# A decode step with three token mixers on one core: the delta rule's preparation written as one run in the order table

## The chip, the cores and the metric

The kernel runs on one core of a Trainium2 chip. The metric is the device time of one execution in microseconds; lower is better. Times are the median of repeated runs, and one further execution was taken with the hardware profiler. Engines are named as in the profile: PE (TensorE, the matmuls), PEld (its weight loads), DVE (VectorE), ACT (ScalarE), POOL (GpSimd) and SP (SyncE, which here only issues DMAs). TensorE's granted clock has two levels, 1.2 and 2.4 GHz; the profile gives it as a share of full speed, 0.50 or 1.00.

## The reference

One decoder layer is computed for a prompt of 256 tokens and for 8 sampled sequences with one new token each (264 columns in all), D_MODEL 1024. Cut to what matters:

```python
h = rms_norm(x, norm1_w) * (1 + sc1) + sh1            # sc, sh from silu(c) @ ada_w
proj = h @ w_in                                        # 22 chunks of 128 columns, and beta/decay columns
u_pool, q_a, k_a, v_a, q_d, k_d, v_d, z, b_raw, a_raw = split(proj)
y_pool = pool_mixer(u_pool)                            # trailing windows 2/4/8/16
q_a, k_a = rms_norm(q_a, q_norm_w), rms_norm(k_a, k_norm_w)     # per head of 64
y_att = moba_attention(q_a, past_k + k_a, past_v + v_a)         # 8 heads; 1024 cached keys a sample
q, k, v = silu(short_conv(q_d, k_d, v_d)); q, k = l2_norm(q), l2_norm(k)
# gated delta rule, 4 heads: in each chunk, with decay from cumsum(g)
A = I + strict_lower(kbeta @ k.T * decay)              # inverted by the triangular solve
u, kcum = solve(A, v * beta), solve(A, kbeta * exp(gcum))
attn = (q @ k.T) * decay                               # then the state is carried over chunks
x = x + g1 * (concat(y_pool, y_att, y_dn) @ w_out)
x = x + g2 * ((silu(h2 @ w_gate) * (h2 @ w_up)) @ w_down)
```

## The kernel before

Activations stand transposed, 128 features on the partitions and 264 token columns. Large operands pass through a ring of five slots of 1 MB (`ring`): column blocks of the weights, and the cached keys and values in pieces of four pages. SP issues their DMAs in the order in which the items are used, and item number n waits until item n-5 was read.

The middle of the program, between the first modulation and the output projection, is one list of steps, the string `ORDER` (L86). Each engine walks the list and issues its own part of a step, if it has one; so the list sets the order on PE, DVE and ACT at once, and also the order of the ring's items (L91 to L99). Every engine runs strictly in order, and semaphores join the parts. There are eight PSUM banks; `opened` makes PE wait until the earlier content of a bank was read. The steps that matter here:

- `W` n, two chunks of the input projection: PE 32 fp32 matmul records (16 matmuls) from a ring slot into banks 0 and 1, ACT copies them out. W5 and W6 hold the last value projections, W0 the pooling columns.
- `K` n, a key item, DVE alone: multiply a ring slot of cached keys with the query (L943, 128x2048), and sum over the head's 64 (L1063). There are 16 of them; nothing needs their result before `OWN`, late in the list. Their ring slots come free when DVE has multiplied.
- The delta rule's preparation: `DSUM` and `DNORM` (L2 norm of its q and k; the first spread of DNORM has ten matmuls on the identity ahead of it in bank 4, `keep_awake`), `GN` (`dn_heads`: betas and decays turned to tokens, spread of the betas into `kbT`, and the products `P1` for the cumulated decay), `GC` (cumulated decays), `GBC` (their spread, the decay matrix), `ROWS` (keys and values turned), `KK` (products of the keys and queries, first triangular factor).
- `KSUM`, `KNORM`: norm of the attention's new keys. `KR`, `KROW`: their rows. `VR`, `VROW`: rows of the new values. `TAILS`: rows for the state outputs.
- `TI`, then `L` s and `M` s for s from 1 to 6: the inverse by doubling. L s: PE multiplies, ACT copies (L1714). M s: PE multiplies, DVE subtracts (L943, six instructions).
- `S`, `H` h: the prompt's attention by heads. In H h PE makes the scores of the next head, then a number of matmuls on the identity given in a table (14, 8, 2, 16, ... for h = 0, 1, 2, 3; in `att_turn`), then waits for the normalised probabilities (`probs`, from DVE's part of H h) and turns them. DVE's part of H h is the normalisation of head h and the mask of head h+1.
- `A` n: modulation columns. PE 16 matmuls from two ring items and four transposes after ACT's copy, DVE a short reduction.
- `OWN`, `DMAX`, `DEXP`, then `V` q: choice of key blocks, softmax over the cached keys, and the value pages, from the ring.

After the list come the output projection and the FFN, with weights split in two parts.

The lines that set the wait for the spread of the delta rule's norm and the wait of a head's transposes are these:

```python
def keep_awake(b, n):
    if n and frees[b]:
        pe.wait_ge(bank_free[b], frees[b])
    for _ in range(n):
        mm(bank[b][:, 0:P], ident[:, :], ident[:, :])
# att_turn(h), after its identity matmuls:
pe.wait_ge(sem("probs"), h + 1)
```

## Time and profile before

| | us |
|---|---|
| median of 3 runs | 591.93 |
| lowest, highest | 591.51, 597.29 |
| the profiled execution | 592.36 |
| its span, first to last instruction | 590.6 |
| mean granted TensorE clock | 0.945 |
| PE busy | 536.5 (91%) |
| DVE busy | 350.1 (59%) |
| ACT busy | 164.4 (28%) |

The table sets the whole execution beside the busy time of its engines. A busy share is a mean over stages; where the program is bound in one stage is read from the idle times in it and from what ended them. In a timeline row the bracket is the engine's idle time ahead of the row and the instruction that ended it. Times in the text are microseconds from the span's start.

### The profile page before, as it was taken

The numbers are of one execution on the slowest core, as the hardware profiler recorded it, in microseconds if no ns is written. First come the engines' busy times: TensorE is split into PE (matmuls) and PEld (weight loads), VectorE is DVE, ScalarE is ACT, GpSimd is POOL, SyncE is SP. The second block draws the span as 40 slices with busy tenths as digits, with TensorE's granted clock in tenths as the row PEclk, the third lists the DMA queues.
The fourth block names the chain that finished last, engine by engine and source line by source line (L and its number), as shares of the span: only waits on it lengthen the run. The fifth ranks groups of instructions, "written<-read, shape, count | busy, mean of one in ns | idle before, by whom it ended". The sixth has DMA issues, their size and how long they took to land.

```text
span 590.6 us, 10244 instructions
## 1 busy us (share of the span) xinstructions
PE 536.5 (91%) x3943; PEld 450.6 (76%) x3943; DVE 350.1 (59%) x550; ACT 164.4 (28%) x233; POOL 55.7 (9%) x125
## 2 busy tenths in 40 slices
PE   7889999897997889888699689888999999999997
PEld 6567767674796767666464169688999999999996
DVE  4441578576987979854753556555664665555441
ACT  4102114512033212221001133462434343423420
POOL 6800000000107500000101000000000000000000
PEclk8879998996799999999888799997999999999999
DMA  9996574294087658462569997684556564545201
GB/s 292 339 306 199 175 248 156 73 246 162 19 273 246 220 175 283 148 205 84 180 215 378 369 321 234 213 267 144 166 192 191 166 198 146 192 155 185 74 18 38
DMA packets 98919, 116.53 MB, mean 197 GB/s; under 512 B 6301, under 2 KB 81262, under 8 KB 98854
## 3 DMA queue, kind: packets, MB, share of 16 engines
q1 hardware_dynamic: 93218, 104.42, 55.3%
q10 hardware_dynamic: 3908, 7.42, 3.5%
q0 software_dynamic: 1744, 4.04, 2.6%
q8 instruction: 31, 0.51, 0.3%
q14 instruction: 18, 0.15, 0.1%
HBM read 113.04 MB, written 2.99 MB: 196 GB/s over the span
## 4 chain that ended last, share of the span: by engine, by line
PE 68%; DVE 19%; DMA 6%; ACT 3%; issue 2%; ACTq 1%; DVEq 0%
PE bank L336 64%; DVE prod L943 4%; DVE s_all L1063 4%; DVE mats L943 3%; DMA ring<-in_ada_w_dram 2%; DMA ring<-in_w_out_dram 2%; DVE BTP L943 1%; DVE cv L1171 1%; DMA ring<-in_cache_v_dram 1%; DMA x_nat<-in_x_sample_dram 1%; PE bank L373 1%; ACT w_part L1752 1%; PE bank L382 1%; PE bank L544 1%; DVE w_ab L943 0%
## 5 line engine op out<-in xcount | busy, mean ns | idle before, releaser
L336 PE MATMUL bank<-a_hi,w_part 128*128 128x264 f32 x832 | 154.4, 287 | 2.1 <-DVE a_lo L1508 2.1
L943 DVE TENSOR_TENSOR w_part<-ring,w_part 128x2048 fp32r<-128x2048 f32 (+1 forms) x38 | 84.9, 2236 | 90.2 <-ACT w_part L1752 90.2
L336 PEld LDWEIGHTS bank<-a_hi,w_part 128*128 128x128 f32 x832 | 130.6, 191 | 2.6 <-issue 2.6
L336 PE MATMUL bank<-a_lo,w_part 128*128 128x264 f32 x416 | 118.9, 286 | 0.0
L1752 ACT ACTIVATE w_part<-ring 128x2048 fp32r<-128x2048 f32 (+1 forms) x38 | 70.9, 1871 | 86.9 <-PE bank L336 75.0
L336 PE MATMUL bank<-hT,ring 128*128 128x264 f32 x352 | 84.3, 398 | 1.8 <-ACT proj L1599 1.8
L336 PEld LDWEIGHTS bank<-hT,ring 128*128 128x128 f32 x352 | 67.7, 195 | 16.1 <-issue 4.5
L336 PEld LDWEIGHTS bank<-a_lo,w_part 128*128 128x128 f32 x416 | 79.5, 191 | 0.1
L336 PE MATMUL bank<-hid_hi,w_part 128*128 128x264 f32 x352 | 64.9, 285 | 0.0
L336 PEld LDWEIGHTS bank<-hid_hi,w_part 128*128 128x128 f32 x352 | 54.5, 188 | 0.1
L336 PEld LDWEIGHTS bank<-ident 128*128 128x128 f32 x344 | 47.3, 219 | 9.3 <-issue 5.6
L336 PE MATMUL bank<-ident 128*128 128x128 f32 x344 | 50.4, 307 | 2.8 <-POOLq L1845 1.9
L336 PE MATMUL bank<-hid_lo,w_part 128*128 128x264 f32 x176 | 49.7, 282 | 0.0
L943 DVE TENSOR_TENSOR prod<-ring,qb 128x2048 f32<-128x2048 f32 x16 | 36.4, 2275 | 3.4 <-ACTq L1643 2.9
L1063 DVE TENSOR_REDUCE s_all<-prod 128x32 f32<-128x2048 f32 x16 | 36.6, 2286 | 0.5
L336 PEld LDWEIGHTS bank<-hid_lo,w_part 128*128 128x128 f32 x176 | 33.1, 188 | 0.0
L1599 ACT ACTIVATE proj<-bank 128x264 f32<-128x264 f32 x22 | 8.6, 390 | 78.5 <-PE bank L336 78.4
L336 PE MATMUL bank<-ring,cT 128*32 128x256 f32 x384 | 24.4, 393 | 4.7 <-DMA ring<-in_ada_w_dram 4.7
L336 PE MATMUL bank<-mats,BTP 128*128 128x128 f32 x192 | 25.0, 280 | 3.4 <-DVEq L1129 2.9
L336 PEld LDWEIGHTS bank<-mats,BTP 128*128 128x128 f32 x192 | 22.9, 191 | 5.2 <-issue 4.1
L336 PE MATMUL bank<-ring,prod 128*32 128x512 f32 x128 | 19.0, 679 | 5.2 <-DMA ring<-in_cache_v_dram 5.2
L336 PEld LDWEIGHTS bank<-ring,cT 128*32 128x32 f32 x384 | 11.3, 112 | 14.0 <-DMA ring<-in_ada_w_dram 5.3
(333 smaller groups left out, 576.4 us busy)
## 6 DMA issues: line engine op xcount, KB each, us to landing
ring<-in_ada_w_dram SPq DMA_DIRECT2D x24, 1024.0 KB, 7.1
ring<-in_cache_k_dram SPq DMA_DIRECT2D x64, 256.0 KB, 3.7
ring<-in_w_in_dram SPq DMA_DIRECT2D x11, 1024.0 KB, 5.4
ring<-in_w_gate_dram SPq DMA_DIRECT2D x11, 1024.0 KB, 5.3
ring<-in_w_up_dram SPq DMA_DIRECT2D x11, 1024.0 KB, 5.3
ring<-in_cache_v_dram SPq DMA_DIRECT2D x40, 256.0 KB, 4.3
ring<-in_w_down_dram SPq DMA_DIRECT2D x8, 1024.0 KB, 5.1
ring<-in_cache_v_dram ACTq DMA_DIRECT2D x24, 256.0 KB, 5.2
```

Source lines behind the costliest of these rows:

```text
L336: return pe.matmul(out, lhsT, rhs, start=start, stop=stop, skip_group_check=True)
L373: last = pe.transpose(b[:, n * P:(n + 1) * P], ada_flat(j)[:, n * P:(n + 1) * P], ident[:, :])
L382: pe.transpose(b[:, r * P:(r + 1) * P], x_nat[:, r, c * P:(c + 1) * P], ident[:, :])
L544: last = pe.transpose(b[:, n * P:(n + 1) * P], sm[:, h % 2, n * P:(n + 1) * P], ident[:, :])
L943: return v.tensor_tensor(out, a, b_, op)
L1063: ins = v.tensor_reduce(s_all[:, o:o + PGI * H], prod[:, :].rearrange("p (g d) -> p g d", d=HD), AX, ALU.add)
L1171: v.scalar_tensor_tensor(out=cv[:, c, back:T], in0=proj[:, CV0 + c, 0:T - back], scalar=cw(i, c), in1=cv[:, c, back:T], op0=ALU.mult, op1= ...
L1599: freed(a.activation(proj[:, j, :], b[:, 0:NT], ACT.Copy), f"proj{j}")
L1752: inc(a.activation(w_hi[:, n % PARTS, 0:c], arrived(a, item)[:, 0:c], ACT.Copy), "w_high")
```

## The change

`ORDER` is another list, and `dn_heads` is cut in two. The new step `KB` (`dn_betas`) takes the spread of the betas and the product `kbT` out of `GN`, on PE and on DVE; `GN` keeps the turning of the heads and the products `P1`, which now follow at once. In the list:

- W4 stands ahead of K3, and GN ahead of DNORM; DVE therefore does K3, GN, DNORM, GC, KSUM, KB, GBC, ROWS, KK without K4, K5, KNORM or KR between them, and PE does W4 to KK without W5 or KNORM.
- K4, W5, KNORM, TI, K5, KR follow behind KK. KSUM stands between GC and GBC.
- W6 follows L1; M1 stands ahead of VR and KROW; L2, K7, M2 ahead of VROW and W0; K8 and L3 ahead of TAILS and S.
- K9 precedes M3 and K10 follows H0; K11 stands between M4 and H1. From H1 on the two lists agree.

Numbers of instructions are the same on PE, DVE, POOL and SP; ACT has two more, both loads of a function table.

```diff
-    ORDER = ("W1 W2 QS W7 K0 CEXT W8 K1 QSUM W9 K2 QNORM W10 CONV BA AB W3 DSUM K3 W4 DNORM KSUM K4 GN W5 "
-             "K5 GC KNORM GBC KR ROWS KK W6 K6 TI VR L1 K7 KROW W0 K8 M1 VROW L2 K9 M2 TAILS L3 S K10 M3 A4 "
-             "H0 K11 L4 M4 H1 A5 H2 L5 K12 M5 A6 H3 K13 H4 L6 K14 M6 POOL H5 UA A7 K15 H6 UB UC H7 UD A8 HE OWN "
...
+    ORDER = ("W1 W2 QS W7 K0 CEXT W8 K1 QSUM W9 K2 QNORM W10 CONV BA AB W3 DSUM W4 K3 GN DNORM GC KSUM KB GBC ROWS "
+             "KK K4 W5 KNORM TI K5 KR L1 W6 K6 M1 VR KROW L2 K7 M2 VROW W0 K8 L3 TAILS S K9 M3 A4 H0 K10 L4 M4 K11 "
+             "H1 A5 H2 L5 K12 M5 A6 H3 K13 H4 L6 K14 M6 POOL H5 UA A7 K15 H6 UB UC H7 UD A8 HE OWN A9 DMAX DEXP V0 "
...
@@ def dn_heads(): (PE)
                 closed(last, "gn")
+
+            def dn_betas():
                 for c in range(GC):
                     b = opened(f"bbc{c}", 5 + c)
@@ def dn_heads(_): (DVE)
                 v.sem_inc(sem("gn_out"), 1)
+                for n in range(TT):
+                    last = tt(P1[:, n, :, :], bc(triu[:, :].unsqueeze(1), [P, GH, P]),
+                              bc(gn[:, n, 1, :].unsqueeze(2), [P, GH, P]), ALU.mult)
+                inc(last, "ug")
+
+            def dn_betas(_):
                 for c in range(GC):
                     b = full(v, f"bbc{c}")
...
                 v.sem_inc(sem("kbT"), 1)
-                for n in range(TT):
-                    last = tt(P1[:, n, :, :], bc(triu[:, :].unsqueeze(1), [P, GH, P]),
-                              bc(gn[:, n, 1, :].unsqueeze(2), [P, GH, P]), ALU.mult)
-                inc(last, "ug")
...
+                "KB": dn_betas
```

First place, PE behind W4 (its two last groups into banks 0 and 1 stand just ahead). `ident,smpT` is GN, `ident` with ten matmuls and the four `rbc,sel8` are DNORM, `mixT,headsum` is KSUM, `smpT,sel8` the spread of the betas, `hT,ring` W5. Before:

```order
L336 MATMUL bank4<-ident 128x128 x10
L336 MATMUL bank4<-rbc,sel8 128x264
L336 MATMUL bank5<-rbc,sel8 128x264
L336 MATMUL bank6<-rbc,sel8 128x264
L336 MATMUL bank7<-rbc,sel8 128x264
L336 MATMUL bank2<-mixT,headsum 8x264 x4
L579 MATMUL bank4<-ident,smpT 128x4 x4
L336 MATMUL bank5<-smpT,sel8 128x264
L336 MATMUL bank5<-smpT,sel8 128x8
L336 MATMUL bank6<-smpT,sel8 128x264
L336 MATMUL bank6<-smpT,sel8 128x8
L336 MATMUL bank0<-hT,ring 128x264 x8
```

Now, with `gn,triu` and `gn,ones` as GC and `BTP1,ones` as GBC:

```order
L579 MATMUL bank4<-ident,smpT 128x4 x4
L336 MATMUL bank4<-ident 128x128 x10
L336 MATMUL bank4<-rbc,sel8 128x264
...
L336 MATMUL bank7<-rbc,sel8 128x264
L336 MATMUL bank7<-gn,triu 128x4
L336 MATMUL bank7<-gn,ones 128x4
...
L336 MATMUL bank2<-mixT,headsum 8x264 x4
L336 MATMUL bank5<-smpT,sel8 128x264
...
L336 MATMUL bank6<-smpT,sel8 128x264
...
L336 MATMUL bank4<-BTP1,ones 128x512
L336 MATMUL bank5<-BTP1,ones 128x512
L609 MATMUL bank6<-ident,cv 128x128 x4
```

W5 is gone from here, and GN has moved ahead of the ten matmuls, into the bank that they write; bank 7 goes from the last spread of DNORM straight to GC.

Second place, PE behind the products of KK (`cv` into bank 7 is the last of them). Before:

```order
L336 MATMUL bank7<-cv 128x128 x4
L336 MATMUL bank0<-hT,ring 128x264 x8
L336 MATMUL bank1<-hT,ring 128x264 x8
L630 MATMUL bank4<-ident,mats 128x128 x4
L630 MATMUL bank5<-ident,mats 128x128 x4
L472 MATMUL bank2<-ident,proj 8x128 x4
L336 MATMUL bank4<-mats,BTP1 128x128 x4
L336 MATMUL bank5<-mats,BTP1 128x128 x4
L480 MATMUL bank2<-ident,proj 128x128 x4
```

Now:

```order
L336 MATMUL bank7<-cv 128x128 x4
L336 MATMUL bank0<-hT,ring 128x264 x8
L336 MATMUL bank1<-hT,ring 128x264 x8
L336 MATMUL bank2<-rbc,sel8 128x264
L336 MATMUL bank3<-rbc,sel8 128x264
...
L632 MATMUL bank4<-ident,mats 128x128 x4
L632 MATMUL bank5<-ident,mats 128x128 x4
L472 MATMUL bank2<-ident,proj 8x128 x4
L336 MATMUL bank4<-mats,BTP1 128x128 x4
...
L336 MATMUL bank0<-hT,ring 128x264 x8
```

W5 and KNORM (`rbc,sel8`) stand between KK and TI (`ident,mats`); W6 stands behind L1 (`mats,BTP1`).

Third place, DVE from the mask of head 1 (in H0) to the normalisation of head 1 (in H1); `prod<-ring` is the first half of a key item, `mats<-mats,bank` the subtractions of M4. Before:

```order
L943 TENSOR_TENSOR smpT<-bank1,cmask 128x384
...
L943 TENSOR_TENSOR prod<-ring,qb 128x2048
L1063 TENSOR_REDUCE s_all<-prod 128x32
L943 TENSOR_TENSOR BTP1<-mats,lvl 128x512
L943 TENSOR_TENSOR mats<-mats,bank6 128x512
L943 TENSOR_TENSOR mats<-mats,bank4 128x512
...
L943 TENSOR_TENSOR mats<-mats,bank5 128x512
L1083 RECIPROCAL st4<-st4 128x2
```

Now:

```order
L945 TENSOR_TENSOR smpT<-bank1,cmask 128x384
...
L945 TENSOR_TENSOR prod<-ring,qb 128x2048
L1065 TENSOR_REDUCE s_all<-prod 128x32
L945 TENSOR_TENSOR BTP1<-mats,lvl 128x512
L945 TENSOR_TENSOR mats<-mats,bank6 128x512
L945 TENSOR_TENSOR mats<-mats,bank4 128x512
...
L945 TENSOR_TENSOR mats<-mats,bank5 128x512
L945 TENSOR_TENSOR prod<-ring,qb 128x2048
L1065 TENSOR_REDUCE s_all<-prod 128x32
L1085 RECIPROCAL st4<-st4 128x2
```

A second key item, K11, has come between M4 and the normalisation of head 1, for which PE waits; the one ahead of M4 is now K10.

## Rows read from the trace of the kernel before

**Rows 1.** The page: the chain that ended last, by line, shares of the span.

```profile
PE bank L336 64%; DVE prod L943 4%; DVE s_all L1063 4%; DVE mats L943 3%; DMA ring<-in_ada_w_dram 2%; DMA ring<-in_w_out_dram 2%; DVE BTP L943 1%; DVE cv L1171 1%; DMA ring<-in_cache_v_dram 1%; DMA x_nat<-in_x_sample_dram 1%; PE bank L373 1
```

**Rows 2.** Windows view: span, busy PE, PEld, DVE, ACT, POOL, granted clock, DMA share, GB/s.

```profile
119.30:213.70 94.40, 82.76 (x521) 68.33 (x519) 77.78 (x97) 19.25 (x41) 23.40 (x39) 0.91 0.63 197
```

**Rows 3.** Timeline of DVE, K3 to S: start, length, instruction, idle before.

```profile
117.03 2.29 DVE L1063 TENSOR_REDUCE s_all<-prod 128x32 f32<-128x2048 f32 x1
121.07 1.69 DVE L1198 SCALAR_TENSOR_TENSOR cv<-cv,bank 128x264 f32<-128x264 f32 x4 [1.75 <-PE bank L336]
124.75 1.79 DVE L1018 RECIPROCAL rbc<-rbc 8x264 f32<-8x264 f32 x1 [2.00 <-ACTq L1657]
126.47 2.22 DVE L943 TENSOR_TENSOR prod<-ring,qb 128x2048 f32<-128x2048 f32 x1
128.72 2.29 DVE L1063 TENSOR_REDUCE s_all<-prod 128x32 f32<-128x2048 f32 x1
...
145.80 0.69 DVE L943 TENSOR_TENSOR mats<-bank,gs 128x512 f32<-128x512 f32 x1 [1.71 <-ACT w_ab L1698]
...
150.39 1.39 DVE L943 TENSOR_TENSOR mats<-mats,triu 128x512 f32<-128x512 f32 x2
...
154.37 0.69 DVE L943 TENSOR_TENSOR mats<-bank,mats 128x512 f32<-128x512 f32 x1 [0.66 <-PE bank L336]
...
158.00 1.29 DVE L943 TENSOR_TENSOR BTP<-mats,lvl 128x512 f32<-128x512 f32 x2
...
191.42 0.56 DVE L943 TENSOR_TENSOR smpT<-bank,cmask 128x384 f32<-128x384 f32 x1 [2.17 <-PE bank L336]
```

**Rows 4.** Timeline of PE: DNORM's identity matmuls, W5, the rest of KNORM.

```profile
117.92 2.39 PE L336 MATMUL bank<-ident 128*128 128x128 f32 x20
...
125.77 7.39 PE L336 MATMUL bank<-hT,ring 128*128 128x264 f32 x32
...
139.23 2.12 PE L336 MATMUL bank<-rbc,sel 8*128 8x264 f32 x4 [4.20 <-DVE proj L1038]
```

**Rows 5.** Timeline of ACT: a table load and what follows it.

```profile
104.89 1.28 ACT L1686 ACT_TABLE_LOAD   x1
106.19 0.52 ACT L1686 ACTIVATE smpT<-smpT,eps 4x264 f32<-4x264 f32 x1
```

**Rows 6.** Windows view by single microseconds, columns as in rows 2.

```profile
136.00:137.00 1.00, 0.00 (x0) 0.00 (x0) 0.97 (x2) 0.00 (x0) 0.00 (x0) 0.57 1.09 389
146.00:147.00 1.00, 1.00 (x8) 0.84 (x6) 0.89 (x2) 0.00 (x0) 0.00 (x0) 0.81 0.00 0
213.00:214.00 1.00, 0.00 (x0) 0.00 (x0) 0.74 (x3) 0.00 (x0) 0.00 (x0) 1.00 0.00 0
```

**Rows 7.** Timeline of PE in the first modulation: a pause, matmuls as in A, its transposes.

```profile
34.55 1.94 PE L336 MATMUL bank<-ring,cT 128*32 128x256 f32 x16 [2.65 <-DMA ring<-in_ada_w_dram]
36.42 1.12 PE L373 MATMUL bank<-ident,adaS 128*128 128x128 f32 x4
```

**Rows 8.** Timeline of PE around H1 and A5.

```profile
206.18 1.16 PE L336 MATMUL bank<-mats,BTP 128*128 128x128 f32 x8 [0.53 <-ACTq L1716]
...
208.96 1.06 PE L336 MATMUL bank<-BTP,mats 128*128 128x128 f32 x8
...
214.56 0.55 PE L544 MATMUL bank<-ident,smpT 128*128 128x128 f32 x3 [1.71 <-DVE smpT L1085]
...
215.84 1.93 PE L336 MATMUL bank<-ring,cT 128*32 128x256 f32 x32
218.58 0.63 PE L373 MATMUL bank<-ident,adaS 128*128 128x128 f32 x4 [0.81 <-ACTq L1580]
```

**Rows 9.** Timeline of DVE at the same place: M4, H1, A5.

```profile
209.14 0.69 DVE L943 TENSOR_TENSOR BTP<-mats,lvl 128x512 f32<-128x512 f32 x1
...
213.76 0.17 DVE L1083 RECIPROCAL st<-st 128x2 f32<-128x2 f32 x1 [0.22 <-DVE mats L943]
...
219.24 0.31 DVE L979 TENSOR_REDUCE modT<-bank 128x36 f32<-128x144 f32 x1 [3.42 <-PE bank L373]
```

More of the change, by code:

```diff
@@ L75, in build @@
     stream = [("ada", i) for i in range(2 * D // IW)]
-    ORDER = ("W1 W2 QS W7 K0 CEXT W8 K1 QSUM W9 K2 QNORM W10 CONV BA AB W3 DSUM K3 W4 DNORM KSUM K4 GN W5 "
-             "K5 GC KNORM GBC KR ROWS KK W6 K6 TI VR L1 K7 KROW W0 K8 M1 VROW L2 K9 M2 TAILS L3 S K10 M3 A4 "
-             "H0 K11 L4 M4 H1 A5 H2 L5 K12 M5 A6 H3 K13 H4 L6 K14 M6 POOL H5 UA A7 K15 H6 UB UC H7 UD A8 HE OWN "
-             "A9 DMAX DEXP V0 XA V1 XB V2 XC V3 XD V4 MX V5 V6 MW0 V7 VE MD MW1").split()
+    ORDER = ("W1 W2 QS W7 K0 CEXT W8 K1 QSUM W9 K2 QNORM W10 CONV BA AB W3 DSUM W4 K3 GN DNORM GC KSUM KB GBC ROWS "
+             "KK K4 W5 KNORM TI K5 KR L1 W6 K6 M1 VR KROW L2 K7 M2 VROW W0 K8 L3 TAILS S K9 M3 A4 H0 K10 L4 M4 K11 "
+             "H1 A5 H2 L5 K12 M5 A6 H3 K13 H4 L6 K14 M6 POOL H5 UA A7 K15 H6 UB UC H7 UD A8 HE OWN A9 DMAX DEXP V0 "
+             "XA V1 XB V2 XC V3 XD V4 MX V5 V6 MW0 V7 VE MD MW1").split()
     ORDER = [(st.rstrip("0123456789"), int("0" + st.lstrip("ABCDEFGHIJKLMNOPQRSTUVWXYZ"))) for st in ORDER]
@@ L817, in _ @@
                 "VROW": lambda _: kv_rows("vrow", VC0, "proj_out", out_count(VC0 + AC - 1)),
-                "GN": lambda _: dn_heads(), "GC": lambda _: dn_cumulate(), "GBC": lambda _: dn_spread(),
+                "GN": lambda _: dn_heads(), "KB": lambda _: dn_betas(), "GC": lambda _: dn_cumulate(), "GBC": lambda _: dn_spread(),
                 "ROWS": lambda _: dn_rows(), "KK": lambda _: dn_products(), "TI": lambda _: dn_first(),
@@ L1465, in _ @@
                 "VR": lambda _: rows8("v8", 2, "v_rows8"), "K": scores, "CEXT": cached_rows, "CONV": convolve, "AB": decays,
-                "DNORM": key_norm, "GN": dn_heads, "GC": dn_cumulate, "GBC": dn_spread, "ROWS": dn_rows, "KK": dn_products,
+                "DNORM": key_norm, "GN": dn_heads, "KB": dn_betas, "GC": dn_cumulate, "GBC": dn_spread, "ROWS": dn_rows, "KK": dn_products,
                 "M": outer, "S": att_first, "H": att_head, "HE": lambda _: att_take(H // 2 - 1), "POOL": pool_maps,
```

## The prediction

> **What bounds the kernel now.** I read the page first: PE is busy 91% of the span by the table above, but the chain that ended last is 64% in PE's matmuls and has DVE's key items, `prod` and `s_all`, as its next two lines [rows 1]. So somewhere both engines take turns. The windows view finds where: from 119.3 to 213.7, the stretch in which the two lists differ, the span is 94.4, PE is busy 82.8 and DVE 77.8 [rows 2]. Neither is full, and neither has more than a fifth of slack. What both do there is the same set of steps before and now (all of K4 to K11, M1 to M4, W5, W6, W0), so the change can give only idle time back: at most DVE's 94.4 - 77.8 = 16.6, of which some 4 are the small gaps between dependent instructions that stay.
>
> Next the timelines. DVE waits 1.75 for the spread of DNORM, 2.00 for ACT's root, 1.71 for ACT's exponential in GBC, 2.17 for the scores of S [rows 3]; PE waits 4.20 for KNORM, which DVE does only behind K5 [rows 4]. The single-microsecond windows show the second price of that last wait: the granted clock falls to 0.50 at 136.4 while PE stands still, and is back only at 146.4 [rows 6]. From 139.23, when PE works again, to 146.4 it ran at 1.2 GHz and lost half of 7.2, that is 3.6. Three pauses are to be kept in mind: 4.20 and, early on, 2.65 ended at 0.50 [rows 4, 6, 7]; 1.71 at 214 did not [rows 6, 8].
>
> **The change, step by step.** Times are those of the span of before; the two programs agree until W4 ends on PE (117.92, where DNORM's identity matmuls began [rows 4]) and K3 ends on DVE (119.32 [rows 3]).
>
> DNORM: its ten identity matmuls write bank 4, which GN now fills just ahead, so PE waits until DVE, behind K3, has copied GN: 119.6. Before, DVE began 3.15 after PE's first such matmul (121.07 - 117.92), so now at 122.75; `P1`, 1.3, fits into the gap. DNORM ends at 124.5, not 122.8. GC shares bank 7 with DNORM's last spread, so PE starts it only then: 0.9, and DVE is through at 125.8. ACT's exponentials take 0.4; then KSUM's root needs another table, 1.28, and 0.5 for itself [rows 5]: 128.1. DVE, in order, waits and takes its reciprocal, 1.79 [rows 3]: 129.8. KB 1.1: 130.9. GBC: 0.6, a wait of 0.5 for ACT's exponential where 1.71 was waited at the low clock [rows 3], 0.7 and 0.7: 133.5. From GBC's second subtraction to the start of KK it was 4.6 with KR's 0.7 in it (145.80 to 150.39), now 3.9 from 132.1: 136.0. KK took from 150.39 to 159.2, 0.66 of it waiting for its last product [rows 3]; PE has that product in time now, so 8.1, and DVE is through the preparation at 144.0 instead of 159.2. Of these 15.2 most is work that only went behind: K4 and K5 at 4.57 each [rows 3], KNORM about 2, KR 0.7. Saved are 3.3 of waiting.
>
> Here the Trainium skill speaks against the change. The load's row is 1.28 long and the next ACTIVATE starts 0.02 after its end [rows 5]. The page "ScalarE: Activation LUTs", section "What ACT_TABLE_LOAD costs", gives the load the same 1.28 but adds a drain of about 1.38, 2.66 a switch; by that KSUM's root, which DVE waits for, would come 1.4 later and the sum would be 1.4 more. The row shows no drain, so I keep 1.28. The second new load, for GBC's exponential, ends at 129.3, ahead of its data, and is hidden.
>
> KNORM, TI: PE has done KK at 138 and W5, 7.2 (125.77 to 133.0 [rows 4]), at 145.1, and makes two of KNORM's spreads. The other two need the banks read, and on DVE K4 stands ahead: 144.0 + 4.6 = 148.6. PE idles from 146.2 to 149.1, 2.9. KNORM ends at 150.8. TI, KR and L1 (two ACT copies) reach 152.9 on PE, W6 160.1, so M1 starts on DVE at 161.0 behind K5, KR, K6.
>
> M1 to S: M1 takes 4.6 (209.14 to 213.76 [rows 9]) and VR 0.7: 166.4. VR's rows hold bank 2 until then, so KROW and all of PE waits from 164.3, 2.1. Then PE's chain is KROW 0.9, L2 1.8, M2 3.6, VROW 0.9, W0 7.2, L3 1.8, TAILS 1.6, S 0.9 (0.11 to 0.12 a record of 128x128, as in M4's groups [rows 8]): 185.1. DVE has done K7, M2 and K8 at 180.2 and waits 4.9. Before, its part of S began at 191.42 [rows 3]; now 6.3 earlier, but with K9 still to do, and one key item stays behind from there to H1. K9 and M3 reach 195.7, A4 and H0 198.2; before, H0 ended at 204.5 with K10 done. So 6.3 ahead, less one item's 4.6. H1 begins at 198.2 + 4.6 (K10) + 4.6 (M4) + 4.6 (K11) = 212.0, against 213.76 [rows 9]. **First term: -1.75.** PE starts work on such steps as soon as it can, and ring items are asked for in the new order, W4 ahead of K3 and A4 ahead of K10; SP issues both at least 10 ahead of their use in this walk, so I cost the reordered queue at nothing.
>
> H1: M4's matmuls start 1.7 after H0's end (206.18 against 204.5) and PE then has 6.7 of work to the end of H1's identity matmuls, of which the row after shows 1.71 of waiting (206.18 to 214.56 [rows 8]). Now 199.9 + 6.7 = 206.6, while the probabilities come 0.8 after H1 begins on DVE: 212.8. PE stands still 6.2 because K11 is in the way. By the pause of 4.20 [rows 4, 6] the clock falls. The chain then goes over H1's transposes and head 0's product, A5's matmuls, its transposes, to DVE, which waits for them 3.42 already [rows 9]. A5's 16 matmuls take 1.93, its transposes 0.63 [rows 8]; at 0.50 eight such matmuls took 1.94, so 16 take 3.9, and the transposes 1.12 [rows 7]. Extra: 0.5 + 0.8 for the first two, 1.9, 0.4. **Second term: +3.6.** Later steps hide what is left of the low clock, since K12 on DVE covers PE.
>
> The pause of 2.9 at KNORM: if the clock falls there, 3.6 is lost as in 139 to 146, in a chain that PE sets as far as S. If it fell already in the thin stretch 129 to 135 (pauses of 0.9 and 1.9), W5 ends later, fills the pause, and about 1.0 is lost; nothing, if it holds. The rows near it are 2.65, which fell, and 1.71, which did not. **Third term: +2.2,** between 0 and 3.6. The pause of 2.1 at KROW is costed at nothing, with 0 to 3.6 kept for the range.
>
> Behind H1 nothing absorbs a shift: the chain runs through DVE's key items and A's matmuls, and the value pages wait for `DEXP`. Sum against the profiled execution of 592.36: -1.75 + 3.6 + 2.2 = 596.4. That execution was 0.4 above the median, so I forecast 596.0.
>
> **Rivals.** *The clock holds.* 1.71 did not fell it [rows 6, 8], and the identity matmuls ahead of H1 fill part of each pause. Then only the first term is left, 590.6 on the profiled execution, 590.2. Against it stands 6.2 of pause. Chance 0.2.
>
> *Faster.* The preparation no longer sets anything: if PE also keeps 2.4 GHz from 133 to 150, W5 and W6 run ahead, S's 4.9 on DVE shrinks, and half of DVE's 12.6 of real waiting is saved: 591.9 - 6.5 = 585.4. For it: the 3.6 lost in the stretch from 139 is on the chain of before. Against: S waits for W0, which is now behind M2. Chance 0.12.
>
> *Slower, by one mechanism: PE paced by DVE loses its clock each time.* The third pause, at KROW, falls as well, in the chain that decides S, and KNORM's in full: -1.75 + 3.6 + 3.6 + 3.6 = +9.0, 601. It decides from a pause between 1.7 and 2.65; KROW's is 2.1. Chance 0.28. Forecast 0.4.
>
> **How the numbers follow.** A measurement here tells about 1% from no change: 586.0 to 597.9. Faster: the second rival, 0.12. Slower: the third rival and the upper part of the forecast's own spread, 0.28 + 0.07 = 0.35. Within 1%: 0.53. Range: half the faster case is left out below, and a fifth of the slower above: 587.5 to 602.5.
>
> **What would show it.** Right: DVE ends KK near 144 with three waits of 1.0 to 2.4 between K3 and KB; PE waits about 2.9 inside KNORM, 2.1 ahead of KROW, DVE 4.9 ahead of S; PE waits about 6 for H1's probabilities, and the clock is 0.50 in A5. Wrong: H1 begins on DVE before 210 or after 216 (the walk is off), or the clock is 1.00 behind the long wait (second term gone), or PE never idles at KNORM.

## The result, and the profile after

The changed kernel takes 604.9 us (median of 4 runs, 602.39 to 606.4); the kernel before, run beside it, 593.09 (4 runs). The ratio is 1.0184, with a 95% interval of 1.0117 to 1.025. Measured again in the last series but one it took 603.16 (4 runs, 599.29 to 606.59), ratio 1.0168 (1.0092 to 1.0243). It is slower, and above the forecast's range of 587.5 to 602.5. (Ratios here and below leave out runs over 1.5% above the fastest of the same kernel, medians are of all runs.) The kernel before spreads by some 5 us to either side, so a ratio needs many runs.

The profiled execution took 606.4, its span is 604.7. The chain that ended last, by line, looks like that of before [rows 1]: the page doesn't show where the time went.

```profile
PE bank L336 66%; DVE prod L945 3%; DVE s_all L1065 3%; DMA ring<-in_ada_w_dram 2%; DMA ring<-in_w_out_dram 2%; DVE mats L945 2%; DVE cv L1173 1%; DMA x_nat<-in_x_sample_dram 1%; DVE BTP L945 1%; PE bank L382 1%; PE bank L373 1%; ACT w_part L1756 1%; PE bank L544 1%; PE bank L480 0%; DVE cv L1175 0%
```

The timeline of DVE does. These rows answer to [rows 3, 9]; columns are start, length, instruction, idle before. The row at 115.05 is K3, that at 149.46 is K4, which follows the preparation's last product, that at 167.67 begins M1, and that at 216.16 is K11.

```profile
115.05 2.22 DVE L945 TENSOR_TENSOR prod<-ring,qb 128x2048 f32<-128x2048 f32 x1
...
123.03 1.76 DVE L1200 SCALAR_TENSOR_TENSOR cv<-cv,bank 128x264 f32<-128x264 f32 x4 [1.79 <-PE bank L336]
126.72 0.17 DVE L1228 COPY gs<-bank 128x16 f32<-128x16 f32 x1 [1.92 <-PE bank L336]
...
130.88 1.79 DVE L1020 RECIPROCAL rbc<-rbc 8x264 f32<-8x264 f32 x1 [3.79 <-ACTq L1661]
...
149.46 2.28 DVE L945 TENSOR_TENSOR prod<-ring,qb 128x2048 f32<-128x2048 f32 x1
...
167.67 0.69 DVE L945 TENSOR_TENSOR BTP<-mats,lvl 128x512 f32<-128x512 f32 x1 [0.63 <-PE bank L336]
...
193.71 0.56 DVE L945 TENSOR_TENSOR smpT<-bank,cmask 128x384 f32<-128x384 f32 x1 [5.61 <-PE bank L336]
...
216.16 2.29 DVE L945 TENSOR_TENSOR prod<-ring,qb 128x2048 f32<-128x2048 f32 x1 [0.22 <-DVE mats L945]
218.49 2.29 DVE L1065 TENSOR_REDUCE s_all<-prod 128x32 f32<-128x2048 f32 x1
220.81 0.17 DVE L1085 RECIPROCAL st<-st 128x2 f32<-128x2 f32 x1
...
229.03 0.31 DVE L981 TENSOR_REDUCE modT<-bank 128x36 f32<-128x144 f32 x1 [6.16 <-PE bank L373]
```

And PE's, for [rows 4, 8] and [rows 7]. In order: the pause ahead of DNORM's identity matmuls, the pause ahead of GC, KSUM, W5, the pause at KROW, the pause at H1's transposes, A5's matmuls and A5's transposes.

```profile
119.86 2.50 PE L336 MATMUL bank<-ident 128*128 128x128 f32 x20 [1.16 <-DVE gn L1209]
...
124.94 0.46 PE L336 MATMUL bank<-gn,triu 128*128 128x4 f32 x2 [0.61 <-DVE cv L1200]
...
126.61 3.69 PE L336 MATMUL bank<-mixT,headsum 128*8 128x264 f32 x8
...
143.79 9.92 PE L336 MATMUL bank<-hT,ring 128*128 128x264 f32 x32
...
173.26 1.94 PE L480 MATMUL bank<-ident,proj 128*128 128x128 f32 x8 [2.58 <-DVE nat L1049]
...
221.62 0.90 PE L544 MATMUL bank<-ident,smpT 128*128 128x128 f32 x3 [6.33 <-DVE smpT L1087]
...
223.92 3.64 PE L336 MATMUL bank<-ring,cT 128*32 128x256 f32 x32
228.37 0.63 PE L373 MATMUL bank<-ident,adaS 128*128 128x128 f32 x4 [0.81 <-ACTq L1584]
```

The windows view gives the clock that goes with them (columns as in rows 2, the granted clock third from the end): down from 125 to 139, again from 142 to 149, from 173 to 176, and through A5.

```profile
125.00:126.00 1.00, 1.00 (x6) 1.00 (x6) 0.00 (x0) 0.00 (x0) 0.00 (x0) 0.53 1.37 192
138.00:139.00 1.00, 1.00 (x6) 0.67 (x6) 0.89 (x4) 0.00 (x1) 0.00 (x0) 0.65 0.00 0
142.00:143.00 1.00, 1.00 (x7) 1.00 (x7) 0.97 (x2) 0.00 (x0) 0.92 (x2) 0.56 0.00 0
148.00:149.00 1.00, 1.00 (x4) 0.79 (x3) 0.97 (x3) 0.00 (x0) 0.00 (x0) 0.53 0.00 0
173.00:174.00 1.00, 0.74 (x4) 0.77 (x5) 0.78 (x2) 0.00 (x0) 0.00 (x0) 0.50 1.04 371
226.00:227.00 1.00, 1.00 (x16) 0.40 (x8) 0.00 (x0) 0.00 (x0) 0.00 (x0) 0.50 0.00 0
```

From here on all executions are compared by four distances on DVE, because they begin the stretch with an offset: K3's product starts between 112.3 and 117.0 in the profiles, though the kernels hardly differ up to there. Where the clock was low in the first modulation differs too. The distances are K3's product to the end of the preparation ("prep"), K3's product to the mask in S ("S"), S to H1's reciprocal ("S-H1"), H1's reciprocal to A5's reduction ("H1-A5"). For before they come from K3's product at 114.78 and from [rows 3, 9]; for after from the rows above: 149.46 - 115.05 = 34.4, 193.71 - 115.05 = 78.7, 220.81 - 193.71 = 27.1, 229.03 - 220.81 = 8.2. The two rows of before that [rows 3] lack are K3's product and the item behind its preparation:

```profile
114.78 2.22 DVE L943 TENSOR_TENSOR prod<-ring,qb 128x2048 f32<-128x2048 f32 x1
...
159.21 2.29 DVE L943 TENSOR_TENSOR prod<-ring,qb 128x2048 f32<-128x2048 f32 x1
```

| | prep | S | S-H1 | H1-A5 | K3 to A5 |
|---|---|---|---|---|---|
| before | 44.4 | 76.6 | 22.3 | 5.5 | 104.5 |
| the forecast's walk | 29.2 | 70.3 | 26.9 | 9.1 | 106.3 |
| after | 34.4 | 78.7 | 27.1 | 8.2 | 114.0 |
| after, second profile | 31.0 | 76.1 | 27.1 | 8.2 | 111.4 |

"After" is the changed kernel; its second profile is that of run e4_changed_again below. The walk's last distance is the 5.5 of before and the 3.6 of the second term; the third term (+2.2, KNORM) is not in that line. After is 9.5 late at A5, and still 9.3 at the first page of values. The second profile is 7.0 late. The two differ by 3.4 in the preparation, where the clock was at 0.50 for some 14 us in the first and some 3 in the second, and by 0.9 the other way behind it. A further 3.3 that the first profile loses in the value part (between the first and the fifth page of values) does not come back in the second, so I don't count it to the change. The windows of this stretch, before, after, and after in its second profile:

```profile
302.26:328.35 26.09, 23.99 (x224) 10.85 (x223) 13.34 (x20) 2.89 (x4) 2.80 (x4) 0.91 1.01 366
```

```profile
311.86:341.20 29.34, 26.96 (x224) 11.89 (x223) 13.37 (x20) 2.89 (x4) 2.79 (x4) 0.83 0.95 329
```

```profile
310.84:336.93 26.09, 24.02 (x224) 10.85 (x223) 13.34 (x20) 2.89 (x4) 2.79 (x4) 0.91 1.02 363
```

The second profile takes exactly the 26.09 of before, and its span of 597.6 is then only 5.3 longer than that of before, counted from K3. That execution took 599.29, inside the forecast's range, but it was the fastest of its four; one execution can't decide.

The DMA queue that the forecast costed at nothing is settled by the same timelines: between K3 and A5 neither PE nor DVE has a wait that a DMA ended.

### The profile page after: what moved, and what is told of

Read it like the earlier page. It is cut to its first block, busy times and chain, and to the rows that moved or that the text cites. A ratio compares the mean times of both kernels' runs of the same rounds, so it can differ in the third digit from the quotient of the medians.

```text
span 604.7 us, 10246 instructions
## 1 busy us (share of the span) xinstructions
PE 544.0 (90%) x3943; PEld 452.2 (75%) x3943; DVE 350.5 (58%) x550; ACT 167.0 (28%) x235; POOL 54.7 (9%) x125
## 4 chain that ended last, share of the span: by engine, by line
PE 70%; DVE 17%; DMA 5%; ACT 3%; issue 2%; SPq 1%; ACTq 0%; DVEq 0%
PE bank L336 66%; DVE prod L945 3%; DVE s_all L1065 3%; DMA ring<-in_ada_w_dram 2%; DMA ring<-in_w_out_dram 2%; DVE mats L945 2%; DVE cv L1173 1%; DMA x_nat<-in_x_sample_dram 1%; DVE BTP L945 1%; PE bank L382 1%; PE bank L373 1%; ACT w_part L1756 1%; PE bank L544 1%; PE bank L480 0%; DVE cv L1175 0%
## 5 line engine op out<-in xcount | busy, mean ns | idle before, releaser
L336 PE MATMUL bank<-hT,ring 128*128 128x264 f32 x352 | 85.6, 403 | 1.7 <-ACT proj L1603 1.7
L336 PEld LDWEIGHTS bank<-ident 128*128 128x128 f32 x344 | 43.7, 205 | 10.5 <-issue 5.6
L336 PE MATMUL bank<-ident 128*128 128x128 f32 x344 | 46.9, 293 | 3.9 <-POOLq L1849 1.9
L336 PE MATMUL bank<-ring,cT 128*32 128x256 f32 x384 | 26.0, 414 | 5.1 <-DMA ring<-in_ada_w_dram 5.1
L336 PE MATMUL bank<-ring,prod 128*32 128x512 f32 x128 | 21.1, 731 | 3.4 <-DMA ring<-in_cache_v_dram 3.4
```

The costliest lines, as they stand in the source:

```text
L336: return pe.matmul(out, lhsT, rhs, start=start, stop=stop, skip_group_check=True)
```

## The experiments

Three theories: T1, TensorE's low clock behind the new pauses is the loss. T2, the order itself is: in-order handovers and key items that come where DVE can't spare the time. T3, the place in question costs nothing.

### First series: one part back at a time

**a1_keys_back**, the changed kernel with K10 out of H1's way:

```diff
- S K9 M3 A4 H0 K10 L4 M4 K11 H1
+ S K9 K10 M3 A4 H0 K11 L4 M4 H1
```

> The changed kernel with the key items behind S put back as in the kernel before (S K9 K10 M3 A4 H0 K11 L4 M4 H1); nothing else. In the changed kernel PE waits 6.3 for H1's probabilities and runs A5 at 0.50; H1 to A5 on DVE takes 8.2 instead of 5.5. Theory 1 (the low clock behind that pause is what it costs): H1 still begins near 221, PE waits under 2 there, A5's matmuls take 1.9 again, and everything behind is 2.7 earlier, ratio to before 1.014. Theory 2 (the wait itself costs, since K11 delays the probabilities): H1 begins 4.6 earlier and the time falls by 4.6 to 7. Theory 3 (this place costs nothing): no change against the changed kernel, ratio 1.018.

Measured 600.92, ratio 1.0116 (1.0062 to 1.017), the branch of T1 for this place. S 78.8, S-H1 27.0, H1-A5 5.5. The pause at H1 is down to 0.74 and with it the low clock in A5 is gone (8.2 to 5.5, worth 2.7), but H1 itself is as late as in the changed kernel: three key items still lie between S and H1, the pause has only moved to H0 (5.40). K9 was not put back ahead of S, so this isn't the tail of before, whatever the run's name and its expectation say.

**a2_awake5**, DNORM's ten identity matmuls in bank 5, so that they need not wait for GN:

```diff
-                keep_awake(banks[0], awake)
+                keep_awake(banks[1] if name == "dn" else banks[0], awake)
```

> The changed kernel with DNORM's ten identity matmuls written into bank 5, which is free, instead of bank 4, which GN holds; nothing else. Theory 1 (the low clock in the preparation, 0.50 from 125.5 to 138.6 and from 142.6 to 149, costs 5.5 of it): the pause of 1.2 ahead of DNORM goes, DNORM starts 1.5 earlier, and if the clock holds the preparation ends 4 to 7 earlier than 149.5. Theory 2 (the handover of banks costs, not the clock): 1.5 earlier and no more. If the clock falls anyway for the pause at GC, 1.5 or less.

Measured 597.27, ratio 1.0095 (1.0053 to 1.0136). Prep 31.8, S 74.7, then 27.1 and 7.0. The pause of 1.16 ahead of DNORM is gone. By the medians of the ratios one bank number gives back about half the loss, but its interval overlaps that of the changed kernel, and the profile doesn't prove it: the preparation, in six profiles that leave its bank and order alone (the changed kernel twice, a1, c1, e1, e2), takes 31.0 to 34.5, and 31.8 lies among them.

**a3_clock_held**, identity matmuls in all pauses (16 ahead of GBC, 12 ahead of KK, 20 ahead of KNORM and KROW each, 58 in H1), a2's bank, GC in bank 3:

> The changed kernel in the same order, with PE's pauses filled by identity matmuls: DNORM's in bank 5, 16 ahead of GBC, 12 ahead of KK, 20 ahead of KNORM, 20 ahead of KROW, 58 instead of 8 in H1, all in banks that are free; GC in bank 3 instead of 7. Theory 1 (the clock is the whole loss): preparation ends near 143, S near 186, H1 begins near 212, A5 at full clock, total 589 to 594, ratio to before about 1.00. Theory 2 (the order's own waits are the loss): the clock is 1.00 but H1 begins no earlier than 218, ratio above 1.01. If filling costs PE time, PE waits for nothing at KNORM and KROW and W6 begins later than 159.

Measured 605.56, ratio 1.018 (1.011 to 1.025). It missed, by my own error. The clock was held from 131 to 304, but the fill was twice as long as I had reckoned and became the bound: in H1 58 of them took 13.22, where eight of them and the pause had taken 8.4.

```profile
131.00:304.00 173.00, 159.83 (x1292) 134.62 (x1290) 127.54 (x201) 33.03 (x78) 24.69 (x39) 1.00 0.54 176
```

```profile
216.18 13.22 PE L336 MATMUL bank<-ident 128*128 128x128 f32 x116
```

The row has two records for each instruction: 0.23 an instruction, not 0.12. It says nothing on T1.

**b1_k11_late**, the kernel before with K10 and K11 one place later:

```diff
- S K10 M3 A4 H0 K11 L4 M4 H1
+ S M3 A4 H0 K10 L4 M4 K11 H1
```

> The kernel before with only the last part of the change: S M3 A4 H0 K10 L4 M4 K11 H1, so that K11 stands between M4 and H1; its preparation is untouched. Theory 1: H1 still begins on DVE near 213.8 to 216, PE pauses 6 ahead of its transposes, the clock is 0.50 in A5, and all behind is 2.7 to 4 later: 596 to 597, ratio 1.005. Theory 3 (the place costs nothing): ratio 1.000.

Measured 600.13, ratio 1.0125 (1.0081 to 1.017), though nothing of the preparation is changed. S 76.6 as before; K3 to A5 108.9, 4.4 late: H1 comes 2.2 later on DVE, PE pauses 4.88 for it, and A5 at the low clock adds 2.3. Part of the loss lies in the tail, more in the time (1.0125) than T1 had expected (1.005).

### Second series: the two places

**c1_k9_ahead_of_s**, the changed kernel with K9 ahead of S and the tail of before; the preparation stays one run:

```diff
- W0 K8 L3 TAILS S K9 M3 A4 H0 K10 L4 M4 K11 H1
+ W0 K8 K9 L3 TAILS S K10 M3 A4 H0 K11 L4 M4 H1
```

> The changed kernel with K9 back ahead of S (K8 K9 L3 TAILS S) and the tail from S as before (S K10 M3 A4 H0 K11 L4 M4 H1); the preparation's run stays. Distances on DVE are counted from the start of K3's product: A5's reduction stood 104.5 behind it before and 114.0 in the changed kernel. In the changed kernel DVE waited 5.61 for S with K9 still to do, so PE set the end of S and K9's 4.57 came on top behind it. If this empty wait is the larger part of the loss (T2), A5's reduction moves to about 107 (K9 in the wait, -4.6, and H1 to A5 as before, -2.7) and the time is 3 above before, 596 beside 593. If only the clock of the preparation and of A5 counts (T1), K9's place gives nothing but the last: 111.3, 600. If the place costs nothing (T3): 114, 605.

Measured 593.94 (10 runs), ratio 0.9995 (0.996 to 1.003). The whole loss is gone by moving three key items. DVE did K9 where it had waited 5.61 for S:

```profile
189.72 2.29 DVE L945 TENSOR_TENSOR prod<-ring,qb 128x2048 f32<-128x2048 f32 x1
192.04 2.29 DVE L1065 TENSOR_REDUCE s_all<-prod 128x32 f32<-128x2048 f32 x1
194.86 0.56 DVE L945 TENSOR_TENSOR smpT<-bank,cmask 128x384 f32<-128x384 f32 x1 [0.53 <-PE bank L336]
```

S 78.0, S-H1 23.1, H1-A5 5.5, K3 to A5 106.6, as T2 had expected (107). The preparation was left as it was, and its clock too: 0.50 from 130 to 139, 33.3 long.

**c2_prep_undone**, the changed kernel with the preparation in the old order and all behind KK as changed:

```diff
- W4 K3 GN DNORM GC KSUM KB GBC ROWS KK K4 W5 KNORM TI K5 KR L1 W6 K6
+ K3 W4 DNORM KSUM K4 GN KB W5 K5 GC KNORM GBC KR ROWS KK TI L1 W6 K6
```

> The changed kernel with the preparation in the old order (K3 W4 DNORM KSUM K4 GN KB W5 K5 GC KNORM GBC KR ROWS KK), and everything behind KK as the changed kernel has it, K9 behind S and K11 ahead of H1 included. This is the tail's share of the loss. b1 (before with K10 and K11 one place later) showed +4.4 at A5's reduction and +7 in time. If the run itself is the larger part (T1, clock at 1.2 GHz inside it), this kernel stands near before: reduction at 106 to 108, 594 to 597. If K9 behind S and K11 ahead of H1 are it (T2), it stands at 111 to 114 and 600 to 604.

Measured 602.93, ratio 1.0151 (1.0072 to 1.0231): undoing the run undoes nothing. K3 to A5 is 116.5, worse than T2's 111 to 114, since this middle has no K5 left and DVE waits 5.79 for M1.

**c3_fitted_fill**, a3 with the numbers mended: 5 ahead of GBC, 3 ahead of KK, 5 ahead of KNORM, 8 ahead of KROW, 24 in H1.

> The changed kernel with identity matmuls put into its pauses in fitted numbers: DNORM's ten in bank 5, 5 ahead of GBC, 3 ahead of KK, 5 ahead of KNORM's spreads, 8 ahead of KROW, 24 in H1, GC's sums in bank 3 instead of 7. In a3_clock_held the same places had 16, 12, 20, 20 and 58; the clock was 1.00 from 131 to 304, but one such matmul takes 0.24 and not the 0.12 that I had reckoned, so the fill became the bound (13.2 ahead of H1's transposes, 4 more than the pause). If the low clock is what the change costs (T1), the reduction of A5 comes at 105 to 107 behind K3 and the time is 594 to 597. If the in-order waits are (T2), the clock is near 1.00 from 131 on and still the reduction stands at 110 or later, 599 or more.

Measured 596.22 (10 runs), ratio 0.9998 (0.9961 to 1.0034). The profile is worse than the time: the clock fell at 122 in DNORM all the same (prep 33.0), K3 to A5 is 111.3, T2's branch, while the time is T1's. Its profiled execution of 596.92 began K3 earliest of all, at 112.3. So this run decides nothing between the two.

**c4_combined**, c1 with a2's bank, GC in bank 3, the fill of 5, 3 and 5, 4 ahead of KROW, and VR ahead of M1:

```diff
- K6 M1 VR KROW
+ K6 VR M1 KROW
```

> c1 and the fitted fill of c3 together (5 ahead of GBC, 3 ahead of KK, 5 ahead of KNORM, 4 ahead of KROW, H1 as it is), with VR ahead of M1 so that KROW does not wait for DVE behind M1. If both costs are real and add up (clock in the preparation about 5, K9 4.6, H1 2.7), A5's reduction stands at 101 to 103 behind K3's start, 2 to 3 ahead of before, and the time is 589 to 592. If the gains overlap, it is at 104 to 106 and 593 to 596.

Measured 588.82 (4 runs), ratio 0.9895 (0.9815 to 0.9974). Prep 28.1, S 72.4 with K9 done, K3 to A5 100.6. In this distance the two parts add.

### Third series: one part alone, in the kernel before

**d1_middle_alone** is c2 with K9 and the tail of before.

> c2_prep_undone (preparation in the old order, the changed kernel's order behind KK) with K9 back ahead of S and the old tail from S. What is left of the change is the middle: TI, L1, W6, K6, M1 ahead of VR, KROW behind M1, VROW and W0 late. Distances are from the start of K3's product to A5's reduction on DVE: before 104.5, changed kernel 114.0, c1 106.6, c2 116.5. In c2 DVE waited 5.79 for M1, since K5 is spent inside the preparation, so this middle fits the old preparation badly: if K9's place is worth the same here as in c1 with H1's pause (7.4), it stands at 109 and the time is 597 to 599. If the middle is free and only K9 and K11 cost, it stands at 104.5 to 106 and the time is 593 to 595.

Measured 598.65, ratio 1.013 (1.0066 to 1.0193), K3 to A5 109.95 (expected 109). The same move as in c1 is worth 6.5 here (116.5 to 109.95).

**d2_run_alone** is the kernel before with the run alone, from W6 on unchanged:

```diff
- K3 W4 DNORM KSUM K4 GN W5 K5 GC KNORM GBC KR ROWS KK W6 K6
+ W4 K3 GN DNORM GC KSUM KB GBC ROWS KK K4 W5 K5 KNORM KR W6 K6
```

> The kernel before with the preparation's run alone (W4 K3 GN DNORM GC KSUM KB GBC ROWS KK, then K4 W5 K5 KNORM KR) and from W6 on its own order, K9 ahead of S and K11 ahead of L4 as it was. If the run itself costs (the clock at 1.2 GHz inside it, T1), A5's reduction stands 107 to 109 behind K3 (before 104.5) and the time is 596 to 598. If the loss lies in where the keys stand behind the run (T2), it stands at 103 to 106 and the time is 592 to 595.

Measured 600.56, ratio 1.0134 (1.0069 to 1.0199), K3 to A5 112.9. Both theories missed: I had put K4 and K5 ahead of KNORM, and PE waits there for both.

```profile
160.60 2.12 PE L336 MATMUL bank<-rbc,sel 8*128 8x264 f32 x4 [7.81 <-DVE proj L1040]
```

So it shows the price of that place, and the run by itself stays unmeasured in this form. The changed kernel has K4 alone there.

**d3_run_filled** is d2 with a2's bank, GC in bank 3 and the fill of 5, 3 and 5.

> d2_run_alone with the fitted fill of c3 and c4 (DNORM's identity matmuls in bank 5, GC's sums in bank 3, 5 ahead of GBC, 3 ahead of KK, 5 ahead of KNORM). The clock should be 1.00 over most of 124 to 150, and the preparation's last product about 5 earlier than in the changed kernel. c4 had KK's start 19.9 behind K3's (changed kernel 26.2, before 35.6). If the clock in the run is worth what c4 against c1 says (6.0 with VR's place), A5's reduction stands 4 to 6 earlier than in d2 and the time is 587 to 590; if PE's matmuls between KNORM and S set the pace anyway, 1 to 2 earlier and 591 to 594.

Measured 599.4 (10 runs), ratio 1.0125 (1.0079 to 1.0172), K3 to A5 111.3, 1.6 less than d2: the branch in which PE's matmuls between KNORM and S set the pace anyway. The times expected for both branches (587 to 594) missed, as d2 itself had come out slower than expected.

**d4_combined_again** is c4 in five rounds.

> c4_combined once more, the same kernel in five rounds, for an interval: c4 measured 588.8 against 594.6 (ratio 0.9895, 0.9815 to 0.9974). If the gain at A5's reduction (3.9 by the traces, of which 2.5 were left at the end) is real, the ratio is 0.988 to 0.996; if it was a favourable set of clock falls in the first modulation and in the value part, 0.997 to 1.002.

Measured 591.29 (12 runs), ratio 0.9972 (0.9931 to 1.0014). The same program, K3 to A5 103.8 instead of 100.6. The windows of both from 122 to 137, c4 first:

```profile
122.00:137.00 15.00, 13.87 (x89) 10.43 (x88) 10.22 (x25) 5.95 (x9) 1.33 (x3) 1.00 0.67 183
```

```profile
122.00:137.00 15.00, 14.36 (x66) 10.18 (x64) 7.73 (x20) 5.04 (x8) 0.00 (x0) 0.77 0.56 148
```

In the same time PE did 89 records at 1.00 and 66 at 0.77. Prep is 31.3 in d4 and 28.1 in c4. That is the cleanest price of the clock here: 3.2 in the preparation, 3.2 at A5. The ratio is the branch of the expectation that calls c4's gain a favourable set of clock falls.

### Fourth series: the shares

**e1_k11_behind_h1** moves one key item in the changed kernel:

```diff
- M4 K11 H1 A5
+ M4 H1 K11 A5
```

> The changed kernel with K11 behind H1 instead of ahead of it (M4 H1 K11 A5), nothing else. Distances from K3's product: H1's normalisation 105.8 in the changed kernel (99.0 before), A5's reduction 114.0 (104.5 before). K11 then lies in DVE's wait for A5's transposes (3.42 before) and TensorE's wait for H1's probabilities is 6.3 - 4.6 = 1.7, which did not lower the clock before. If the debt is only paid where DVE would wait anyhow: H1 at 101.2, A5's reduction at 107.3 to 107.8, time 597 to 599. If K11's place matters only by the clock in A5 (T1), A5's reduction comes 2.7 earlier, 111.3, 601 to 602.

Measured 596.28 (10 runs), ratio 1.0032 (0.9989 to 1.0076). S-H1 22.4, H1-A5 6.6: 6.3 of the changed kernel's 35.3 between S and A5 are gone by one item. PE's pause at H1 is 1.67, A5's matmuls take 1.93 again, and K11 lies where DVE had waited:

```profile
216.75 2.29 DVE L945 TENSOR_TENSOR prod<-ring,qb 128x2048 f32<-128x2048 f32 x1
219.08 2.29 DVE L1065 TENSOR_REDUCE s_all<-prod 128x32 f32<-128x2048 f32 x1
221.40 0.31 DVE L981 TENSOR_REDUCE modT<-bank 128x36 f32<-128x144 f32 x1
```

Prep is 34.5, the low clock of the changed kernel's first profile unmended, and still the time is 0.3% above before, 0.8% at most.

**e2_k9_only** moves only K9 (K8 K9 L3 TAILS S M3 A4).

> The changed kernel with K9 ahead of S (K8 K9 L3 TAILS S) and the rest as the changed kernel has it, so K10 behind H0 and K11 between M4 and H1. If the empty wait of 5.61 at S is worth K9's 4.57 and H1's pause with A5 at the low clock is the other 2.7, S stays at 78 to 79 behind K3, H1's normalisation at 101.2 and A5's reduction at 109 to 109.5; time 599 to 600. If the two gains are one and the same (the clock alone), A5's reduction stays at 112 or later, 603.

Measured 597.73 (10 runs), ratio 1.0059 (1.002 to 1.0098), K3 to A5 110.1. S-H1 falls from 27.1 to 24.4, by 2.7 and not by K9's 4.6: with K9 gone DVE waits 1.29 for A4's transposes and the gaps it had covered open. H1's pause is 4.88 and H1-A5 stays at 8.2. So an item taken out of a full stretch need not give back its whole length.

**e3_fill_in_run** is the changed kernel with a2's bank, GC in bank 3, 5 identity matmuls ahead of GBC and 3 ahead of KK:

```diff
             def dn_spread():
+                keep_awake(3, 5)
...
             def dn_products():
+                keep_awake(3, 3)
```

> The changed kernel with the fill inside the preparation only (DNORM's identity matmuls in bank 5, GC's sums in bank 3, 5 ahead of GBC, 3 ahead of KK), none at KNORM, KROW or H1. If TensorE's 1.2 GHz from 125.5 to 149 is part of the loss, the clock is 1.00 over more of it, the preparation ends 3 to 5 earlier behind K3 than the 34.4 of the changed kernel, and A5's reduction stands at 109 to 111, 600 to 602. If PE's work from KNORM to S sets S anyway, S stays at 78 to 79 and A5's reduction at 113 to 114, 604 to 605.

Measured 597.7 (10 runs), ratio 1.0047 (1.0 to 1.0094). Prep 28.1, S 72.2, S-H1 27.1, K3 to A5 106.1. DVE, at the preparation's end and at S, from a K3 at 116.71:

```profile
143.60 1.29 DVE L947 TENSOR_TENSOR BTP<-mats,lvl 128x512 f32<-128x512 f32 x2
144.81 2.28 DVE L947 TENSOR_TENSOR prod<-ring,qb 128x2048 f32<-128x2048 f32 x1
...
188.88 0.56 DVE L947 TENSOR_TENSOR smpT<-bank,cmask 128x384 f32<-128x384 f32 x1 [5.18 <-PE bank L336]
```

That is better than T1's own branch (109 to 111). The walk's sum at A5 comes out (106.3), its parts within 3 (29.2, 70.3, 26.9, 9.1). But the run changes more than the clock: DNORM no longer waits for its bank, which alone brings its products 1.2 forward on DVE (6.8 behind K3 instead of 8.0), and the clock was still at 0.50 from 138 to 142, from 151 to 155 and in A5. ACT's rows decide the question that the forecast had raised on the function table:

```profile
126.61 1.28 ACT L1660 ACT_TABLE_LOAD   x1
127.91 0.47 ACT L1660 ACTIVATE rbc<-bank,eps 8x264 f32<-8x264 f32 x1
```

**e4_changed_again** is the changed kernel, unchanged.

> The changed kernel itself again, for a second profile and more runs: 604.9 median of 4 so far, A5's reduction 114.0 behind K3's product. By both theories 602 to 606; the low stretches of the clock between 120 and 150 will not be the same, and A5's reduction will vary with them by up to 3, as it did between c4 and d4 (100.6 and 103.8), while DVE's wait for S stays at 4 to 6 and H1's pause at 6.3.

Measured 603.16, told above. Prep 31.0, S 76.1; the waits of the order are the same to 0.1 (6.32 at H1) or nearly (5.18 for S). Between K3 and S the clock was down from 127 to 131 and from 151 to 159 only. The second stretch lies behind KNORM's pause. These are PE's rows from there to W6, a window of it, and the start of M1 on DVE:

```profile
152.59 2.12 PE L336 MATMUL bank<-rbc,sel 8*128 8x264 f32 x4 [3.16 <-DVE proj L1040]
154.64 1.97 PE L632 MATMUL bank<-ident,mats 128*128 128x128 f32 x8
...
159.56 7.29 PE L336 MATMUL bank<-hT,ring 128*128 128x264 f32 x32
```

```profile
152.00:153.00 1.00, 0.41 (x1) 0.42 (x2) 0.90 (x3) 0.00 (x0) 0.00 (x0) 0.50 0.99 367
```

```profile
167.84 0.69 DVE L945 TENSOR_TENSOR BTP<-mats,lvl 128x512 f32<-128x512 f32 x1 [2.25 <-PE bank L336]
```

**f1_best** is c4 without the fill at KNORM and KROW.

> e3's fill inside the preparation, c1's order (K9 ahead of S, K11 ahead of L4) and VR ahead of M1, without the fill at KNORM and KROW that c4 had. From K3's product: e3 had S at 72.2 with K9 still to do and waited 5.18 there, so S at 71 to 73 with K9 done; from S to A5's reduction c1 had 28.6: sum 100 to 102, against 104.5 before. Time 589 to 592, ratio 0.990 to 0.997. If TensorE's clock falls in KNORM's or KROW's pause instead (fill left out there), 103 to 105 and 0.997 to 1.003.

The windows of its profile, from K3's product to S and from S to A5's reduction:

```profile
114.48:186.46 71.98, 67.66 (x405) 56.66 (x404) 61.55 (x71) 18.87 (x33) 12.42 (x19) 0.95 0.56 173
186.46:214.67 28.21, 21.76 (x203) 17.51 (x203) 23.06 (x37) 6.21 (x18) 13.54 (x20) 1.00 0.71 234
```

K3 to A5 is 100.2, as expected and 4.3 ahead of before in its profile, and the profiled run took 586.51. Yet the time is 589.9 (12 runs) against 592.58, ratio 0.9989 (0.995 to 1.0027): no difference that can be told, and less than expected. Of the three measurements of this version and its sister only c4's lies below 1 with its whole interval. It is as good as the kernel before, perhaps a little better.

## Why the prediction was wrong

By the forecast's own steps, in distances from K3 and against before:

| | forecast | after | second profile |
|---|---|---|---|
| K3 to S, the lead | -6.3 | | |
| KNORM's low clock, inside K3 to S | +2.2 | 0 | about +2.2 |
| K3 to S, both together | -4.1 | +2.0 | -0.5 |
| S to H1, one key item more | +4.6 | +4.8 | +4.8 |
| H1 to A5, low clock | +3.6 | +2.7 | +2.7 |
| sum at A5 | +4.1 | +9.5 | +7.0 |

And K3 to S by its parts, as lengths (M1's first row on DVE stands at 161.0 in the walk, 167.67 after, 167.84 in the second profile, 164.16 in e3):

| | forecast's walk | after | second profile | e3 |
|---|---|---|---|---|
| K3 to the preparation's end | 29.2 | 34.4 | 31.0 | 28.1 |
| from there to M1 | 17.0 | 18.2 | 20.4 | 19.4 |
| M1 to S | 24.1 | 26.0 | 24.7 | 24.7 |

**The step that failed is the lead in the first term: S done on PE at 185.1, and so "6.3 ahead, less one item's 4.6".** The item's price and the place where it is paid were right. The lead that was to pay for it wasn't there: S came 8.4 later than the walk has it in the first profile (78.7 against 70.3), 5.8 in the second.

- In the preparation, 5.2 and 1.8. The walk costed PE's steps there at 2.4 GHz. In the first profile the clock fell at 125.1, behind pauses of 1.16 and 0.61: KSUM took 3.69, GBC's sums 3.78 (1.88 in e3), W5 9.92 instead of 7.39. e3, c4 and f1 do the same steps in 28.1, all three, with the clock up and without the wait for DNORM's bank; d4, d3 and c3, with the same banks and fill, take 31.3, 32.5 and 33.0, with the clock down again.
- Between its end and M1, 1.2 and 3.4. Of both, 1.2 is a wrong sum: the walk has TI, KR's transposes and L1 on PE in 2.1 (150.8 to 152.9), and at full clock they take 3.3 (156.09 to 159.39 after; as long in the kernel before). The other 2.2 of the second profile is KNORM's low clock.
- Between M1 and S, 1.9 and 0.6. The 1.3 between the two profiles is KROW's low clock, which only the first has.

**KNORM's term (+2.2) was right in one execution and not in the other.** The forecast named 129 to 135 as a thin stretch where the clock might fall, and priced that case at 1.0, the cheapest. In the first profile it was the dear one: from KSUM to KK DVE and PE mostly take turns, and with the clock at 0.50 for 14 us the preparation is 3.4 longer than in the second profile. With W5 slowed to 9.92 the pause in KNORM (2.9 forecast) shrank to 0.21. In the second profile the clock was up again at 131, the pause came, 3.16, and behind it the low clock, at the price forecast.

**The second term was right in kind, and too large:** H1's pause 6.33 (6.2 forecast), clock 0.50 in A5's matmuls, which took 3.64 (3.9). A5's transposes ran at full clock again (0.63), which the forecast had at 1.12. Cost 2.7, not 3.6. a1, c1 and e1 each take the pause away, and 1.6 to 2.7 with it.

**KROW's pause** (2.1 forecast, costed at nothing) was 2.58. The clock fell there in the first profile, from 173 to 176, and not in the second (2.57) nor in e1 (2.58). A pause of that length can go either way; the fall cost 1.3, not the 3.6 kept for the range.

**The table load** was no cost in the changed kernel, where ACT's root waited 1.50 for KSUM's bank instead. In e3 it was on the path with its last 0.3: KSUM's matmuls ended at 127.6, the load at 127.89, and the root followed 0.02 later. The Trainium skill's page "ScalarE: Activation LUTs", section "What ACT_TABLE_LOAD costs", has a drain of about 1.38 besides the load; e3's rows show none, as the forecast had chosen.

**DVE's wait of 5.61 for S stood in the walk, as "waits 4.9".** It was the plainest sign in it, and I read it as slack. An item that is pushed out of an empty wait into a full stretch can cost its whole length: 4.8 here. Between S and H1 DVE has next to no slack; ahead of S it had 5.6.

**The forecast's own signs of being wrong came.** H1 began on DVE at 220.81, behind its 216, and in the first profile PE hardly idled at KNORM.

**The rivals.** The slower one (601, three pauses at the low clock) came nearest in the time. Its mechanism holds in part: in the first profile the clock fell inside the preparation, at KROW and at H1, in the second briefly inside the preparation, at KNORM and at H1, never at all three pauses. It kept the lead at S, less the two pauses, and so came near by luck in part. "Clock holds" fell. "Faster" fell for the changed kernel; c4 and f1 are what it needed, with other places for K9, K11 and VR, and even then only 0 to 1%.

T1 and T2 both hold. At A5, counted from the changed kernel's first profile, moving keys alone gives 7.4 (c1), banks and fill alone 7.8 (e3), both, with VR moved, 13.4 (c4); from its second profile 4.8, 5.3 and 10.8. These are single profiles. In the time the two do not add: keys alone bring the ratio to 0.9995, banks and fill alone to 1.0047, and the three measurements of both together, with VR moved, lie at 0.9895, 0.9972 and 0.9989. So moving key items is enough to repair the loss, and how much of the changed kernel's 2% is the clock's isn't shown to better than this. T3 fell for K9 and K11. What stays open besides: what the run costs with the middle of before, since d2 put K5 in the wrong place, and why the clock falls in one execution of a program and not in the next.
